# Closing stage of each layer: the second row set of the expert sums is added by accumulating transfers instead of by VectorE

## What is computed

```python
f = _moe(tokens, ...)            # routed experts (8 of 64 per token) + one shared expert
x = x + g2 * _rms_norm(f[:n_lat].reshape(bsz, s_len, dm), post_ffn_g[l])
if with_ctx:                     # layer 0 only
    xc = xc + g2c * _rms_norm(f[n_lat:].reshape(bsz, -1, dm), post_ffn_g[l])
```

## Time and profile before

| | us |
|---|---|
| median of 3 runs | 2919.43 (2918.8 to 2921.94) |
| the profiled execution, its own time | 2917.33 |
| span of the profiled execution | 2915.5 |
| closing stage of layer 0, from the first issue on SP (1596.52) to the end of the last L1812 (1628.65) | 32.1 |
| closing stage of layer 1, from 2887.78 to the end of the last L1812 (2912.07) | 24.3 |
| TensorE matmul busy | 2595.9 |
| VectorE busy | 1081.1 |
| ScalarE busy | 588.0 |
| GpSimd busy | 390.1 |

### The profile page before, as it was taken

The page is one execution under the profiler, slowest core; times in us unless marked ns, Lnnn a source line. Parts: engine busy times, 40 slices in busy tenths (PEclk is TensorE's granted clock), DMA queues, the critical chain, the costliest instruction groups (busy, mean ns, idle before and its releaser), DMA issues. The chain is left out here.

```text
span 2915.5 us, 44582 instructions
## 1 busy us (share of the span) xinstructions
PE 2595.9 (89%) x13635; PEld 1267.2 (43%) x13636; DVE 1081.1 (37%) x3197; ACT 588.0 (20%) x1379; POOL 390.1 (13%) x312
## 2 busy tenths in 40 slices
PE   7999989896899999999996588989978999899894
PEld 3566555543433333333332266666533333333331
DVE  3443360515333333333332643451433332233233
ACT  2323241402011111111111341331310111111111
POOL 1000001001022222221221200001010212112212
PEclk9999999997999999999998799999989999999997
DMA  7120303007478998999993402202156999998983
GB/s 275 50 91 30 130 12 132 32 13 287 169 236 301 353 327 284 324 325 334 328 367 81 188 1 90 87 34 96 37 215 235 361 397 392 389 391 297 388 313 106
DMA packets 104979, 619.27 MB, mean 212 GB/s; under 512 B 22832, under 2 KB 23088, under 8 KB 64688
## 3 DMA queue, kind: packets, MB, share of 16 engines
q1 hardware_dynamic: 71184, 530.30, 46.2%
q0 software_dynamic: 33696, 87.63, 12.3%
HBM read 578.84 MB, written 77.99 MB: 225 GB/s over the span
## 5 line engine op out<-in xcount | busy, mean ns | idle before, releaser
L1513 PE MATMUL ps<-wgu,xT 128*64 128x512 f32 x3584 | 808.0, 604 | 43.1 <-DMA wgu<-in_exp_gu 34.2
L1513 PEld LDWEIGHTS ps<-wgu,xT 128*64 128x64 f32 x3584 | 253.8, 139 | 502.2 <-issue 492.2
L1522 PE MATMUL ps<-wd,hiddenT 128*64 128x512 f32 x1824 | 420.3, 603 | 11.2 <-issue 10.8
L624 PE MATMUL ps<-w_in,hT 128*128 128x512 f32 (+5 forms) x1152 | 369.0, 479 | 14.7 <-PEq L574 3.8
L1442 POOL DMA_INDIRECT ffn_rows<-Y,six x114 | 182.6, 1602 | 1110.8 <-issue 635.3
L1695 DVE TENSOR_TENSOR hidden<-silu,ps 128x256 f32<-128x256 f32 x112 | 47.2, 421 | 704.3 <-ACT silu L1631 698.5
L624 PEld LDWEIGHTS ps<-w_in,hT 128*128 128x128 f32 x1152 | 218.0, 196 | 155.7 <-issue 136.0
L1522 PEld LDWEIGHTS ps<-wd,hiddenT 128*64 128x64 f32 x1824 | 123.2, 137 | 227.7 <-issue 227.7
L1631 ACT ACTIVATE silu<-ps 128x256 f32<-128x256 f32 x112 | 43.1, 385 | 797.7 <-PE ps L1513 797.7
L1626 ACT ACTIVATE Y<-ps,wc 128x512 f32<-128x512 f32 x114 | 78.4, 688 | 417.4 <-PE ps L1522 417.4
L1689 DVE TENSOR_SCALAR Y<-ps,wc 128x512 f32<-128x512 f32 x114 | 85.6, 751 | 198.4 <-PE ps L1522 198.4
(11 more groups left out here) (490 smaller groups left out, 2724.1 us busy)
## 6 DMA issues: line engine op xcount, KB each, us to landing
wgu<-in_exp_gu SPq DMA_DIRECT2D x128, 2048.0 KB, 22.9
wd<-in_exp_d SPq DMA_DIRECT2D x128, 1024.0 KB, 8.2
ada_start<-in_ada_w SPq DMA_DIRECT2D x8, 1024.0 KB, 8.0
w_in<-in_w_in SPq DMA_DIRECT2D x4, 2048.0 KB, 10.8
w_in<-in_w_out SPq DMA_DIRECT2D x4, 2048.0 KB, 12.4
aw_0A<-in_ada_w SPq DMA_DIRECT2D x6, 1024.0 KB, 4.8
aw_0B<-in_ada_w SPq DMA_DIRECT2D x6, 1024.0 KB, 4.8
aw_0C<-in_ada_w SPq DMA_DIRECT2D x6, 1024.0 KB, 4.8
```

The lines of the kernel that those rows point to most:

```text
L624: last = pe.matmul(pp[i % 2][:, at:at + c1 - c0], hT[:, k, i * P:(i + 1) * P], wg[g % 2][:, k, c0:c1], start=(k == 0), stop=(k == KD - 1))
L1513: last = pe.matmul(ps[h * HB:(h + 1) * HB, 0, :], xT[:, k, h * HB:(h + 1) * HB], wgu[w[h]][:, k, :], start=(k == 0), stop=(k == KD - 1))
L1522: last = pe.matmul(ps[h * HB:(h + 1) * HB, 1 + c, :], G[:, f, h * HB:(h + 1) * HB], wd[w[h]][:, f, c * 512:(c + 1) * 512], start=(f == 0), ...
```

## The change

SP no longer loads the second row set, and the tile `f2` is gone. Instead POOL issues, for each tile, a transfer from the second row set in DRAM to `f[:, i, :]` with `accum_op=ALU.add`: the transfer itself adds to what is in `f`. VectorE's `add_halves` is removed, and ScalarE waits for POOL's transfer.

```diff
-    s_f, s_sum = [S(f"ffn_loaded{i}") for i in range(nt)], S("halves_added")
+    s_f = [S(f"ffn_loaded{i}") for i in range(nt)]
+    s_second = [S(f"second_set_added{j}_{l}") for j in range(2)]
...
-        f2 = v.sb(f"second{l}", [P, nt, D], scope=scope)
...
                     sp.dma_start(f[:, i, :], v.acc_dram[i * P:(i + 1) * P, :]).then_inc(s_f[i].sem, 16)
-                    sp.dma_start(f2[:, i, :], v.acc_dram[NROW + i * P:NROW + (i + 1) * P, :]).then_inc(s_f[i].sem, 16)
...
                 for i in range(nt):
-                    s_sum.wait(act, i + 1)
+                    s_second[i % 2].wait(act, 16 * (i // 2 + 1))
                     s_sq.wait(act, i)
...
             @block.gpsimd
             def _(pool):
-                for i in range(nt):
+                def add_second_set(i):
+                    s_f[i].wait(pool, 16)
+                    s_second[i % 2].wait(pool, 16 * (i // 2))
+                    pool.dma_start(f[:, i, :], v.acc_dram[NROW + i * P:NROW + (i + 1) * P, :], accum_op=ALU.add).then_inc(s_second[i % 2].sem, 16)
+
+                for i in range(3):
+                    add_second_set(i)
+                for i in range(nt):
+                    if i + 3 < nt:
+                        add_second_set(i + 3)
                     s_ms.wait(pool, i + 1)
                     pool.tensor_tensor(ss[:, 2, i:i + 1], ss[:, 1, i:i + 1], v.half[:, 0:1], ALU.pow).then_inc(s_rstd.sem, 1)
...
-                def add_halves(i):
-                    s_f[i].wait(dve, 32)
-                    dve.tensor_tensor(f[:, i, :], f[:, i, :], f2[:, i, :], ALU.add).then_inc(s_sum.sem, 1)
-
-                add_halves(0)
-                add_halves(1)
                 mean_square(0)
                 s_row.wait(dve, 16)
                 for i in range(nt):
-                    if i + 2 < nt:
-                        add_halves(i + 2)
                     if i + 1 < nt:
                         mean_square(i + 1)
```

More of the change, by code:

```diff
@@ L1813, in ffn_residual @@
     for s in s_f:
-        s.stage_over(32)
-    s_sum.stage_over(nt)
+        s.stage_over(16)
     for s, k in ((s_row, 16), (s_sq, nt), (s_ms, nt), (s_rstd, nt), (s_x, nt), (s_step, counts[0])):
```

## The result

The changed kernel is slower by 0.28%: the ratio to the kernel before is 1.0028, 95% interval 1.0019 to 1.0037, over 11 runs of each. The medians are 2928.96 and 2918.80 us. 0.28% is 8.2 us (5.5 to 10.8); the ratio is not that of the medians, which lie 10.2 us apart.

What follows compares the result with a forecast made beforehand. Closing stages were taken as bound by the DMA engines first, then VectorE. Layer 0 +4.3 and layer 1 +2.7 us make +7.0 on the median 2919.43: 2926.4 us, range 2920 to 2941.

Steps and rivals of the forecast that it cites:

- What bounds after: Closing stages: DMA engines through the last accumulate, then square, mean square and two VectorE tiles, 6.4 us after landing.
- the sign that was named: Profile after, both closing stages: VectorE waits for ScalarE, and it for accumulating transfers, up to the last two tiles.
- The adds, 7 us gross: VectorE in the closing stages: six of ten removed adds lie on the path, about 1.2 us each.
- The accumulation, 3.0 us per transfer: DMA engines in the closing stages: each 512 KB accumulating transfer takes 3.0 us, against 1.27 plain.
- The 196 GB/s: POOL's transfers alone at the end of layer 0's expert loop, rate at full share; 2.7 us per 512 KB.
- The first accumulate therefore flows at about T + 4.8: POOL's first transfer: data flows 4.8 us after T, the stage's first issue, from a 3.4 us load and 1.3 us start.
- a landing and 1.3 us, together 2.0: POOL's two slots: next transfer needs landing (0.7 us) plus 1.3 us, under the 3.0 us of the one in between.
- Rival 1: Closing stages: accumulating hardly dearer than plain, six adds fall away, about -7 us, 2912.4; chance 0.04.
- Rival 2: Closing stages: 2.7 us per transfer, gain and cost nearly cancel, +4 us, 2923.4; chance 0.30 for 2.1 to 2.85 us.
- Rival 4: POOL's two transfers under way don't fill the engines; 2946 at 5 us each, 2965 at 6.9; chance 0.14.
- Rival 5: VectorE's two-operand SBUF instructions delay POOL's issues, about 0.3 us each, at worst 1.3, +5 us, 2931; chance 0.06.
- `pow` at nothing: POOL's `pow` behind transfer issues: L1810 up to 0.9 us late, covered by the 3.0 us tile period, costing nothing.

Runs made afterwards that it cites:

- f2: Kernel before, second row set loaded by POOL's queue instead of SP's, plain, at most two at a time, VectorE adding; stages 35.54 and 26.06 us, ratio 1.0016.
- f1: Changed kernel without accum_op: the same ten POOL transfers, but plain, overwriting the first set; stages 31.71 and 24.03 us, ratio to the kernel before 0.9966.
- f3: Changed kernel with three accumulating transfers allowed under way in layer 0 instead of two; stages 34.59 and 27.10 us, ratio to the kernel before 1.0014.
- f4: Kernel before, accumulating transfers only for tiles 4 and 5 of layer 0 and tile 3 of layer 1; stages 30.66 and 24.90 us, ratio 0.9985.
- g4: As g3_order, with layer 0's tile 5 alone accumulated, its first set loaded between tiles 2 and 3; stages 29.83 and 22.33 us, ratio 0.9988.
- g1: Changed kernel, SP holding gate rows and loads from tile 3 until POOL's first accumulate landed; stages 38.10 and 27.74 us, ratio to the kernel before 1.0033.
- g3_order: Kernel before, no accumulating transfers, gate rows loaded after tile 1, VectorE's list reordered to finish tile 0 earlier; stages 30.34 and 22.54 us, ratio 0.9988.

## Why the prediction was right

Forecast were +7.0 us in the stages and slower by a little over 0.2%. The stages grew by 6.7 and the time by 8.2 (5.5 to 10.8; the lower end is at that 0.2%). The sum is closer than its parts: layer 0 grew by 3.5 and not by 4.3, layer 1 by 3.2 and not by 2.7, and the two errors cancel. By its steps:

- **What bounds after.** Right in layer 1; in layer 0 the transfers and VectorE end together, and the sign that was named, VectorE waiting for ScalarE up to the last two tiles, did not appear there. Behind the last landing come 6.4 us of square, mean square and two tiles (measured 6.3). The last landing was forecast at 30.0 and 20.15 us into the stages and came at 29.3 and 21.2.
- **The adds, 7 us gross.** f2 against f1 measures them, with the sets on the same queues: 35.54 - 31.71 = 3.8 and 26.06 - 24.03 = 2.0, together 5.9. Within 1.1 of the forecast, though in f1 the second set also waits for the first.
- **The accumulation, 3.0 us per transfer.** The size was read from the whole program's q0 and q1. Measured were 2.9 us in the changed kernel and 2.5 in f3. The 3.0 was right for the kernel as it is, but not as a price of the engines alone. And it was luck in part. It rests on gathers that run at the plain rate. The 196 GB/s that was kept as a bound for the scatters comes from a window in which the gather issued at 1578.44 is under way; if all gathers ran at 196, the same sum would leave 331 GB/s for the scatters, 1.6 us. Nor does a run show why a transfer into SBUF should cost what a scatter into DRAM does. On the path accumulation costs after minus f1, 3.9 + 3.4 = 7.4 us.
- **"The first accumulate therefore flows at about T + 4.8. From there the engines always have plain or accumulating packets."** The first sentence is the step that failed, though the sum did not notice; the second held, since SP's packets filled the engines. The 1.3 us from issue to data were read from a transfer with nothing else on the engines. With SP's transfers queued it was 4.8 us (4.3 in layer 1), so the first one flowed at T + 8.7, and it landed at 13.4 where 8.5 at the soonest was implied (4.8 + 3.0 + 0.7). And "a landing and 1.3 us, together 2.0" was too short: from f1, landing to issue is 0.5 and issue to landing 4.5 with 1.27 of data in it, 3.7 us in all without data. POOL's queue with its two slots, at nothing in the forecast beyond its start, costs f2 minus before, 3.4 + 1.8 = 5.2 us.
- **Why the sum held.** f1 minus f2 (-5.9, the adds), after minus f1 (+7.4, accumulating) and f2 minus before (+5.2, the queue) add up to the +6.7 of the stages, as three differences in a row must; the split is a rough one, since f2's transfers don't wait for the first set as f1's do. The forecast had counted the engines' whole work up to the end of the data, 17 us more of it for ten transfers, and not each transfer's way. While both queues are full, work on the engines is conserved whoever goes first, so the late start of POOL's transfers moved the end of the data little. That is argued from the windows, full until 1630, and not tried by itself. With cheap transfers the late start decides: f1 shows it.
- **Rival 1, VectorE stays the bound, -7 us.** Its mechanism is out for this kernel, and its price was wrong as well. In f1 the transfers are plain and VectorE does run without a wait from tile 0 on, but the stages gain 0.7 us, not 7, because tile 1 lands late.
- **Rival 2, 2.7 us per transfer.** It differs from the forecast by 3 us in the whole; with 2.9 measured the forecast is nearer, but the time alone would not have told them apart.
- **Rival 4, the slots run dry.** Partly true and wrongly judged by its sign. It was to be seen by a share well under 1; the share stayed at 1.04 and a third slot still gave 1.05 us, a fraction of the rival's 20 to 39.
- **Rival 5, VectorE holds up POOL's issue.** Out: the issues took 0.83 to 0.98 us, and tile 0's, with VectorE idle, was the longest. (In f4 one of them took 1.20 us beside L1822.)
- **`pow` at nothing.** Nearly: VectorE waited for it in three tiles of layer 0, 1.6 us in all, and was through with tile 3 just as the last square's sum came, so the end did not move.

The Trainium skill, DMA: Bandwidth & Descriptors, section Issuing engines are not separate DMA queues, says that it saves only the time to issue when several engines start transfers, and that they interleave on the same 16 DMA engines. Both agree with f2: it gained nothing, and once both queues have packets on the engines they take turns (207 and 203 packets from 1600 to 1604). What cost time here is the 4.1 us before POOL's first packet and, behind it, the limit of two.

## What to carry to other kernels

Here an accumulating transfer saved VectorE an add of 1.2 us and cost the DMA engines 2.5 to 2.9 us for 512 KB, where a plain one costs 1.27. It paid for two tiles whose transfers had the DMA engines to themselves and took 5.4 and 6.6 us while VectorE had other tiles to work on (f4 in layer 0), and not for all tiles of a stage that the loads bound. Before a load moves to another queue, ask what is queued on the one it leaves: with SP's loads queued, POOL's first packet came 3.7 to 4.8 us after the issue. And where VectorE waits for loads, look first at what else in its own list could run there: reordering it, with the gate rows one tile later, gained 3.5 us in the stages with the same bytes and the same operations.

## What the runs showed of the hardware that was not expected

- A DMA share of 1.03 to 1.06 is no proof that the engines are at their limit: at that share they moved 182 GB/s of accumulating transfers in the changed kernel and 210 in f3.
- A transfer issued by POOL while SP has loads queued starts late, whatever it does. The first packet of POOL's queue came 4.8 and 4.3 us after the issue in the changed kernel (layers 0 and 1), 3.7 in f1, 4.1 in f2, 4.6 in f3 and 4.3 in g4; with SP held back after three loads it was 1.7 us (g1), and with nothing else on the engines 1.6 (f4). After that the two queues move about as many packets. In layer 0 the first transfer took 9.5 us accumulating and 7.6 plain, 6.1 accumulating in g1. What holds the first packets back was not tried.
- `pow` of one value per row took 0.57 us in the kernel before with VectorE idle, and 1.52 us where L1810 was already running (1.46 in g3_order beside the add to `xs`); it then ended 0.4 us after that instruction.
